# Host-laid feature-major memories, vectors and spatial weights, and a first layer that opens with the projections of raw memory

## Chip, core and metric

The kernel runs on one core of one Trainium2 chip. The metric is the device time in microseconds (us) of one execution. The engines are PE (TensorE), DVE (VectorE), ACT (ScalarE), POOL (GpSimd) and SP (SyncE, which here only issues DMA). The host prepares arrays before the launch; its time is not part of the metric.

## What is computed

Two blocks follow each other on 256 tokens of width 1024, two layers each. The part that matters here is the first block, and in it the branch that attends to a memory of 256 rows:

```python
def hybrid_layer(x, mem, ...):
    h = rms_norm(x, norm_pre)
    proj = h @ w_in                      # queries, keys, values, gates of five branches
    ...
    mkv = rms_norm(mem, mem_norm) @ w_mem_kv
    mem_k, mem_v = jnp.split(mkv, 2, axis=-1)
    y_xa = flat(memory_attention(heads(xa_q), heads(mem_k), heads(mem_v)))
    ...
def spatial_gating(u, v, ln_g, ln_b, w_s, b_s):
    mixed = jnp.einsum('gpq,bnqgc->bnpgc', jnp.where(mask, w_s, 0.0), vb)
```

`rms_norm(mem, g)` is, row by row, `mem * rsqrt(mean(mem^2) + eps) * g`. The factor of a row can be applied before or after the product with `w_mem_kv`. The second block has cross-attention to `mem_2` of the same form.

## The kernel before

**Products.** Every float32 weight is split in two fp32r parts, high and low, and a product is three passes: high x high, low x high, high x low. The host order `UNITS` cuts all weights into units of 512 KB. SP loads unit n into slot n mod 8 of `weights_raw` as soon as PE has finished unit n-8. ACT copies it to `weights_hi` (helper `emit`, L583); DVE subtracts and writes `weights_lo` into the same slot (L1056). PE takes the units in order. `proj_T` gives tokens on partitions (L1696), `proj_F` (L1728) and `proj_H` (L1761) features on partitions; in `proj_H` the sums of the two halves of a bank are taken by DVE (`both`, L1110).

**Order.** All four engines run straight lists written by hand; nothing reorders them. Where ACT or DVE wait for a bank (`filled`, `for_tile`) or for each other (`after_act`, `after_vec`), they first emit the splits of the units that their tables say are due:

```python
            def for_tile(name, i, stage=None):
                n, u = PC.split_at((name, i), stage), PC.unit_at((name, i), stage)
                while 0 < n < len(SPLITS) and SPLITS[n] < u + RAW - 2 and (n < SPLIT or SPLITS[n - SPLIT] < u - 1):
                    n += 1
                up_to(n)
```

So a wait inside ACT's list holds back all splits behind it, and SP's loads follow PE.

**Opening of layer 0.** SP loads `x` (two tiles of 512 KB), the identity, units 0 to 7, then 1184 KB of constants. PE runs 9 idle products on zeros (L1843), turns the 8 rows of `norm_pre` into columns (L1853), transposes the normalised tokens (L1815, `norm_T`) and starts on the queries `sbq` (L1728), the keys `sbk` (L1761), the gate columns `mlif` (L1870, L1871) and the values `sbv` (L1696). POOL loads some 40 small rows of vectors, which PE later turns into `vector_columns` (L1865) and `vector_columns_2` (L1929).

**Memory.** POOL loads `mem` as rows; ACT sums the squares (`square`, L621), DVE scales and adds eps (`base`, L1079), ACT takes Ln and Exp (`root`, L625, L627), DVE multiplies the rows (L1089). PE transposes 16 tiles (`turn`, L1801) to `memT`; ACT copies them and forms the high part of memory times `mem_norm`, DVE the low part (L1222). The key projection `mk` of layer 0 runs in the middle of the layer, the value projection `mv` behind `mlz`. Layer 1 does the same with `mem_2`, and the multiplied parts for the second layer and the second block come from `memT` (`mem_gains` L659, `mem_low` L1119). The spatial weights are a unit of 256 KB per layer that PE transposes (L1964).

## Time and profile before

| | |
|---|---|
| time, median of 3 runs | 1752.22 us (1751.6 to 1752.3) |
| span of the profiled execution | 1750.3 us |
| PE busy | 1740.1 us, 99% |
| DVE, ACT, POOL busy | 1283.1, 1024.5, 114.3 us |
| DMA | 306.64 MB, mean 175 GB/s |
| chain that ended last | PE 91%, DVE 6%, ACT 1% |

The only time given for the profiled execution is its span, from its first to its last instruction; the median lies 1.9 us above it, for what stands around the span. Busy shares are averages: the chain of waits tells which engine set the end in a stretch.

### The profile page before, as it was taken

The numbers are of one execution on the slowest core, as the hardware profiler recorded it, in microseconds if no ns is written. First come the engines' busy times: TensorE is split into PE (matmuls) and PEld (weight loads), VectorE is DVE, ScalarE is ACT, GpSimd is POOL, SyncE is SP. The second block draws the span as 40 slices with busy tenths as digits, with TensorE's granted clock in tenths as the row PEclk, the third lists the DMA queues.
The fourth block names the chain that finished last, engine by engine and source line by source line (L and its number), as shares of the span: only waits on it lengthen the run. The fifth ranks groups of instructions, "written<-read, shape, count | busy, mean of one in ns | idle before, by whom it ended". The sixth has DMA issues, their size and how long they took to land.

```text
span 1750.3 us, 24767 instructions
## 1 busy us (share of the span) xinstructions
PE 1740.1 (99%) x9406; PEld 1512.0 (86%) x9406; DVE 1283.1 (73%) x1714; ACT 1024.5 (59%) x1417; POOL 114.3 (7%) x186
## 2 busy tenths in 40 slices
PE   9999999999999999999999999999999999999998
PEld 8988898888889888888889988888888988888887
DVE  6966676665877586757669787688778987678775
ACT  7865566454666655644555765755556656555544
POOL 5000000000000000000000000500003360000000
PEclk9999999999999999999999999999999999999999
DMA  9656654566765566565666664456665515356663
GB/s 303 193 157 178 177 169 151 175 190 186 213 181 160 166 181 175 156 181 169 191 195 197 182 192 157 144 182 193 192 186 186 171 36 181 121 169 188 188 189 109
DMA packets 204070, 306.64 MB, mean 175 GB/s; under 512 B 12362, under 2 KB 100340, under 8 KB 203824
## 3 DMA queue, kind: packets, MB, share of 16 engines
q1 hardware_dynamic: 201056, 298.91, 56.1%
q0 software_dynamic: 2896, 6.15, 1.1%
q8 instruction: 75, 1.23, 0.3%
q14 instruction: 43, 0.35, 0.1%
HBM read 303.97 MB, written 1.05 MB: 174 GB/s over the span
## 4 chain that ended last, share of the span: by engine, by line
PE 91%; DVE 6%; ACT 1%; issue 1%; DMA 0%; DVEq 0%; ACTq 0%
PE bank L1696 52%; PE bank L1761 22%; PE bank L1728 8%; DVE bank L1573 2%; DVE weights_lo L1056 2%; PE bank L1801 1%; PE bank L1815 1%; PE bank L2093 1%; PE bank L2111 1%; PE bank L1823 1%; PE bank L1784 1%; ACT weights_hi L583 1%; PE bank L2017 0%; PE bank L1982 0%; PE bank L2065 0%
## 5 line engine op out<-in xcount | busy, mean ns | idle before, releaser
L1056 DVE TENSOR_TENSOR weights_lo<-weights_raw,weights_hi 128x1024 fp32r<-128x1024 f32 x560 | 668.9, 1233 | 248.6 <-ACT weights_hi L583 243.7
L583 ACT ACTIVATE weights_hi<-weights_raw 128x1024 fp32r<-128x1024 f32 x560 | 574.8, 1056 | 386.0 <-DMA weights_raw<-in_w_in_dram 181.3
L1696 PE MATMUL bank<-weights_hi,h_parts 128*128 128x512 f32 x1856 | 567.6, 391 | 0.4 <-DVE h_parts L1478 0.2
L1696 PEld LDWEIGHTS bank<-weights_hi,h_parts 128*128 128x128 f32 x1856 | 348.1, 188 | 73.3 <-DVE h_parts L1478 0.6
L1696 PE MATMUL bank<-weights_lo,h_parts 128*128 128x512 f32 x928 | 348.0, 390 | 0.0
L1696 PE MATMUL bank<-weights_hi,arena_parts 128*128 128x512 f32 x928 | 270.1, 391 | 0.0
L1761 PE MATMUL bank<-h_parts,weights_hi 128*128 128x512 f32 (+1 forms) x992 | 241.0, 385 | 0.5 <-DVE arena L1110 0.4
L1696 PEld LDWEIGHTS bank<-weights_lo,h_parts 128*128 128x128 f32 x928 | 174.4, 188 | 35.3
L1696 PEld LDWEIGHTS bank<-weights_hi,arena_parts 128*128 128x128 f32 x928 | 173.6, 188 | 35.4
L1761 PEld LDWEIGHTS bank<-h_parts,weights_hi 128*128 128x128 f32 x992 | 175.3, 189 | 31.8 <-DVE arena L1110 0.9
L1696 PE MATMUL bank<-weights_lo,arena_parts 128*128 128x512 f32 x464 | 158.4, 390 | 0.0
L1110 DVE TENSOR_REDUCE arena<-bank 128x256 f32<-128x512 f32 x148 | 102.1, 690 | 66.3 <-PE bank L1761 63.4
L1761 PEld LDWEIGHTS bank<-h_parts,weights_lo 128*128 128x128 f32 x992 | 134.8, 191 | 8.8
L1761 PE MATMUL bank<-h_parts,weights_lo 128*128 128x256 f32 x992 | 138.4, 283 | 0.0
L1728 PE MATMUL bank<-h_parts,weights_hi 128*128 128x256 f32 x768 | 133.7, 284 | 0.0
L1728 PEld LDWEIGHTS bank<-h_parts,weights_hi 128*128 128x128 f32 x768 | 116.3, 192 | 0.2 <-issue 0.2
L1696 PEld LDWEIGHTS bank<-weights_lo,arena_parts 128*128 128x128 f32 x464 | 87.2, 188 | 17.9
L1728 PE MATMUL bank<-h_parts,weights_lo 128*128 128x256 f32 x384 | 99.8, 284 | 0.0
L603 ACT ACTIVATE arena<-bank 128x512 f32<-128x512 f32 x140 | 83.0, 593 | 15.4 <-PE bank L1696 9.0
L1728 PEld LDWEIGHTS bank<-h_parts,weights_lo 128*128 128x128 f32 x384 | 69.7, 192 | 0.2 <-DVE weights_lo L1056 0.2
L960 ACT ACTIVATE arena<-arena,vector_columns 128x256 f32<-128x256 f32 x48 | 28.9, 602 | 64.7 <-DVE arena L1110 64.7
L541 POOL TENSOR_SCALAR arena<-constants_sb,vector_columns 128x128 f32<-128x128 f32 x76 | 35.4, 486 | 390.0 <-PE bank L1696 207.5
(326 smaller groups left out, 1667.6 us busy)
## 6 DMA issues: line engine op xcount, KB each, us to landing
weights_raw<-in_w_in_dram SPq DMA_DIRECT2D x224, 512.0 KB, 3.7
weights_raw<-in_f_w_up_dram SPq DMA_DIRECT2D x96, 512.0 KB, 3.5
weights_raw<-in_f_w_down_dram SPq DMA_DIRECT2D x48, 512.0 KB, 3.6
weights_raw<-in_w_up_dram SPq DMA_DIRECT2D x40, 512.0 KB, 3.5
weights_raw<-in_c_w_pw_dram SPq DMA_DIRECT2D x24, 512.0 KB, 3.6
weights_raw<-in_ab_w_in_dram SPq DMA_DIRECT2D x20, 512.0 KB, 3.8
weights_raw<-in_w_mem_kv_dram SPq DMA_DIRECT2D x16, 512.0 KB, 3.6
weights_raw<-in_w_out_dram SPq DMA_DIRECT2D x16, 512.0 KB, 3.6
```

Source lines behind the costliest of these rows:

```text
L541: ins = nc.gpsimd.tensor_scalar(diag(ft, d), ident, cols2[:, c:c + 1], 1.0, ALU.mult, ALU.mult)
L583: nc.scalar.activation(w_hi[:, q % SPLIT, 0:w], raw[:, n % RAW, 0:w], ACT.Copy).then_inc(hi_done, 1)
L603: link(nc.scalar.activation(dst, (view(b) if view else b[:, :]), func, **kw), ("free", name, i), *marks)
L960: link(nc.scalar.activation(c[:, f, :], feat(2)[:, f, :], ACT.Identity, scale=cols2[:, w0 + 48 + ft:w0 + 49 + ft], bias=cols2[:, b0 + ft:b ...
L1056: tt(w_lo[:, n % RAW, 0:w], raw[:, n % RAW, 0:w], w_hi[:, q % SPLIT, 0:w].bitcast(F32), ALU.subtract)\
L1110: link(nc.vector.tensor_reduce(dst, b, AX.X, ALU.add), ("free", name, f), f"{name}sum{f}")
L1573: stt(dst, feat(2, 2)[:, ft, 0:S - d], cols2[:, c:c + 1], acc[:, j, d:S], ALU.mult, ALU.add)\
L1696: return mm(bs[t][:, :], sp_[:, 2 * u + kk, t * P:(t + 1) * P], wp[:, kk, :], start=first and u == us[0] and kk == 0 and n == 0, stop=last ...
L1728: return mm(bs[i][:, j, :], wp[:, kk, f * P:(f + 1) * P], sp_[:, 2 * u + kk, :], start=first and u == us[0] and kk == 0 and n == 0 and j == 0,
L1761: return mm(out, w[n][:, kk, j * P:(j + 1) * P], sp_, start=u == 0 and kk == 0 and n == 0, stop=u == 1 and kk == 3, skip_group_check=True)
L1784: ins = mm(bs[j][:, 1, :], w[0][:, kk, j * P:(j + 1) * P], src[1][:, k, :], start=False, stop=u == 1 and kk == 3, skip_group_check=True)
L1801: ins = nc.tensor.transpose(b[:, j, t * P:(t + 1) * P], src[:, t, (2 * i + j) * P:(2 * i + j + 1) * P], ident)
```

## The change

The host now lays out seven arrays. `memT` and `mem_2T` are the memories with features first; `columns` and `columns_2` hold all vectors as columns, one load each; `gm_wsT` holds the spatial weights transposed. PE's transposes of these are gone, and so is the unit of spatial weights.

Layer 0 opens with `mk` and `mv` on raw memory times `mem_norm`. DVE forms both parts from three pieces of `memT`. The rows of `mem` are still loaded, for the mean squares alone. Their factors `mem_rstd` multiply the results: `mv` when ACT copies it out of its bank, `mk` on DVE after PE has spread the factors over all partitions (the new tile `mrs`, two small products a layer). DVE also multiplies `memT` itself with them (`memn`), for the later layers.

```diff
...
+        mem_rstd = [st[:, 11, t:t + 1] for t in range(NT)]
...
+            ORDER[f"L{l}"] = (four("mk") + (two("mv") if l == 0 else []) + four("hT") + two("sbq") + four("sbk") + pick("mlif", 0)
+                              + two("sbv") + pick("mrs", 0) + two("sbz") + (two("mv") if l else []) + four("sbs") + two("mlq", "mlk") + four("sbw") + two("mlv")
...
+                else:
+                    ap = kmaj("w_mem_kv", (l,))
+                    got.extend((True, ap[:, 4 * u:4 * u + 4, i * S:(i + 1) * S]) for u in range(2) for i in range(2))
+                    mem_v()
...
+            mT = A["memT"].rearrange("(k p) s -> p k s", p=P)
+            for i, (k0, k1) in enumerate(MEM_PIECES[:2]):
+                sp.dma_start(memT[:, k0:k1, :], mT[:, k0:k1, :]).then_inc(memT_in[i], 16)
             for n, (split, src) in enumerate(UNITS):
                 r = n % RAW
+                if n == 0:
+                    dst = raw[:, 0, 0:W].rearrange("p (k m) -> p k m", k=2)
+                    sp.dma_start(dst, src[:, 0:2, :]).then_inc(first_in, 16)
+                    dst = raw[:, 0, W:2 * W].rearrange("p (k m) -> p k m", k=2)
+                    sp.dma_start(dst, src[:, 2:4, :]).then_inc(raw_full[0], 16)
+                    continue
+                if n == 2:
+                    k0, k1 = MEM_PIECES[2]
+                    sp.dma_start(memT[:, k0:k1, :], mT[:, k0:k1, :]).then_inc(memT_in[2], 16)
+                if n == 4:
+                    for t, s in enumerate((x0_in, x1_in)):
+                        sp.dma_start(xs[:, t, :], A["x"][0][t * P:(t + 1) * P, :]).then_inc(s, 16)
+                    sp.dma_start(cst[:, 0:P], A["constants"][:, 0:P]).then_inc(ident_in, 16)
...
+            pool.dma_start(arena[:, 6:8, :], A["mem"][0].rearrange("(t p) d -> p t d", p=P)).then_inc(mem_in, 16)
...
+                    pool.dma_start(memT[:, :, :], A["mem_2T"].rearrange("(k p) s -> p k s", p=P)).then_inc(mem2T_in, 16)
...
+                    pool.dma_start(cols2[:, :], A["columns_2"]).then_inc(cols2_in, 16)
...
+                pool.dma_start(wsT[:, :, :], A["gm_wsT"][l]).then_inc(ws_in, 16)
...
+            def mem_norm(src):
+
+                for t in range(NT):
+                    for n in range(2):
+                        square(src[:, t, n * 512:(n + 1) * 512], "mem", t, n)
+                for t in range(NT):
+                    act.wait_ge(vec_done, after_vec(f"mem.base{t}"))
+                    link(nc.scalar.activation(mem_rstd[t], st[:, 8, 2 * t + 1:2 * t + 2], ACT.Ln, scale=1.0 / D, bias=st[:, 9, t:t + 1]))
+                    link(nc.scalar.activation(mem_rstd[t], mem_rstd[t], ACT.Exp, scale=-0.5), f"mem.rstd{t}")
...
+                    act.dma_start(cols[:, :], A["columns"]).then_inc(cols_in, 16)
+                    log_exp_table()
+                    up_to(4)
                     act.wait_ge(pool_done, GC.at("eps"))
-                    log_exp_table()
                     for t, s in enumerate((x0_in, x1_in)):
+                        up_to(4 + 2 * t)
                         act.wait_ge(s, 16)
                         link(nc.scalar.activation(sec(21), xs[:, t, :], ACT.Square, accum_out=st[:, 8, t:t + 1]))
                         link(nc.scalar.activation(st[:, 1, t:t + 1], st[:, 8, t:t + 1], ACT.Ln, scale=1.0 / D, bias=epsc))
                         link(nc.scalar.activation(st[:, 1, t:t + 1], st[:, 1, t:t + 1], ACT.Exp, scale=-0.5), f"h.rstd{t}")
-                    copy(cols[:, 0:8], "cols", 0, ACT.Copy, "gain", view=lambda b: b[:, 0:8])
-                    up_to(1)
...
+                    act.wait_ge(mem_in, 16)
+                    mem_norm(rows_of(6))
+                    for t in range(NT):
+                        copy(tok(5)[:, t, :], "mv", t, ACT.Copy, f"mv{t}", scale=mem_rstd[t])
...
+                    hi, lo = M_HL["L0"][:2]
+                    dve.wait_ge(cols_in, 16)
+                    for i, (k0, k1) in enumerate(MEM_PIECES):
+                        dve.wait_ge(memT_in[i], 16)
+                        for k in range(k0, k1):
+                            link(ts(hi[:, k, :], memT[:, k, :], cols[:, 8 + k:9 + k], None, ALU.mult))
+                        for k in range(k0, k1):
+                            link(stt(lo[:, k, :], memT[:, k, :], cols[:, 8 + k:9 + k], hi[:, k, :].bitcast(F32),
+                                     ALU.mult, ALU.subtract), f"m_lo{k}")
+                        if i == 1:
+                            up_to(2)
+                    up_to(4)
+                    all_of(feat(4), "mk", range(4), 2)
                 whole_norm(xs, xn, "h", "xn", based=True)
-                if l:
+                if l == 0:
+                    for t in range(NT):
+                        base("mem", t)
...
+                b = filled("mrs")[:, 0:S].unsqueeze(1)
                 if l == 0:
-                    hi, lo = M_HL["L0"][:2]
-                    for i in range(4):
-                        b = halves(filled("memT", i))
-                        for j in range(2):
-                            k = 2 * i + j
-                            dve.wait_ge(act_done, after_act(f"m_hi{k | 1}"))
-                            link(stt(lo[:, k, :], b[:, j, :], cols[:, 8 + k:9 + k], hi[:, k, :].bitcast(F32),
-                                     ALU.mult, ALU.subtract), *([("free", "memT", i), f"m_lo{i}"] if j else []))
+                    link(tt(feat(4), feat(4), b.to_broadcast([P, 4, S]), ALU.mult), "mk")
...
+                link(tt(memT[:, :, :], memT[:, :, :], b.to_broadcast([P, KD, S]), ALU.mult), "memn", ("free", "mrs", 0))
...
+                    elif opening:
+                        for kk in range(4):
+                            if at[0] == 1 and kk == 0:
+                                pe.wait_ge(first_hi, 1)
+                            if at[0] == 1 and kk == 2:
+                                pe.wait_ge(hi_done, 1)
+                            pe.wait_ge(vec_done, VC.at(f"m_lo{4 * u + kk}"))
+                            for j in range(2):
+                                part(j, kk, 0, bs[j].rearrange("p n s -> p (n s)"), src[2][:, 4 * u + kk].rearrange("p n s -> p (n s)"))
+                        low_half()
...
-                    idle(9)
+                    idle(6)
+                    for u in range(2):
+                        for i in range(2):
+                            proj_H("mk", i, M_HL["L0"], (u,), opening=True)
+                    proj_T("mv", src=M_HL["L0"])
...
-                m = rows_of(17 if l else 6)
-                pe.wait_ge(vec_done, VC.at("mem.n1"))
-                for i in range(4):
-                    turn("memT", i, m)
+                pe.wait_ge(act_done, SC.at("mem.rstd1"))
+                b = begin("mrs")
+                for t in range(NT):
+                    ins = mm(b[:, t * P:(t + 1) * P], mem_rstd[t].to_broadcast([P, P]), ident, start=True, stop=True)
+                end(ins, "mrs")
...
-                w = unit(4, P)
-                b = quarters(begin("wsT"))
-                for g in range(4):
-                    ins = nc.tensor.transpose(b[:, g, :], w[:, g, :], ident)
-                used(ins, ("wsT", 0))```

In the rows of order below, `weights_hi<-weights_raw` is ACT's split of a unit and `weights_lo<-weights_raw,weights_hi` DVE's. The first place is the opening on ACT. Before:

```order
L618 ACT_TABLE_LOAD
L675 ACTIVATE arena,statistics<-x_tokens 128x1024
L676 ACTIVATE statistics<-statistics 128x1
L677 ACTIVATE statistics<-statistics 128x1
L675 ACTIVATE arena,statistics<-x_tokens 128x1024
L676 ACTIVATE statistics<-statistics 128x1
L677 ACTIVATE statistics<-statistics 128x1
L603 ACTIVATE vector_columns<-bank 128x8
L583 ACTIVATE weights_hi<-weights_raw 128x1024
L654 ACTIVATE h_parts<-bank,vector_columns 128x256 x4
L583 ACTIVATE weights_hi<-weights_raw 128x1024
```

Now (L668 to L670 are the sums and factors of `x`, L600 the squares of `mem`, L624 and L625 its factors, L582 the copies of `mv`, L643 the high part of the tokens):

```order
L562 ACTIVATE weights_hi<-weights_raw 128x1024 x2
L668 ACTIVATE arena,statistics<-x_tokens 128x1024
L669 ACTIVATE statistics<-statistics 128x1
L670 ACTIVATE statistics<-statistics 128x1
L600 ACTIVATE spatial_weights,statistics<-arena 128x512 x4
L624 ACTIVATE statistics<-statistics 128x1
L625 ACTIVATE statistics<-statistics 128x1
L624 ACTIVATE statistics<-statistics 128x1
L625 ACTIVATE statistics<-statistics 128x1
L562 ACTIVATE weights_hi<-weights_raw 128x1024 x8
L582 ACTIVATE arena<-bank,statistics 128x512 x2
L643 ACTIVATE h_parts<-bank,vector_columns 128x256 x8
```

The first of these rows are units 4 and 5, the eight splits units 6 to 13: the squares and factors of memory now stand between unit 5 and unit 6, and units 6 to 13 ahead of the parts of the tokens.

The second place is the opening on DVE. Before:

```order
L1172 MEMSET arena 128x256
L1089 TENSOR_SCALAR arena<-x_tokens,statistics 128x1024
L1087 TENSOR_SCALAR arena<-x_tokens,statistics 128x512 x2
L1056 TENSOR_TENSOR weights_lo<-weights_raw,weights_hi 128x1024
L1104 SCALAR_TENSOR_TENSOR h_parts<-bank,vector_columns,h_parts 128x256 x4
```

Now, from the split of units 2 to 4 on (L1084 are the sums of `mk`, L1063 and L1061 the scaled tokens, L1053 the bases of memory's factors):

```order
L1030 TENSOR_TENSOR weights_lo<-weights_raw,weights_hi 128x1024 x3
L1084 TENSOR_REDUCE arena<-bank 128x256 x2
L1030 TENSOR_TENSOR weights_lo<-weights_raw,weights_hi 128x1024
L1084 TENSOR_REDUCE arena<-bank 128x256 x2
L1063 TENSOR_SCALAR arena<-x_tokens,statistics 128x1024
L1061 TENSOR_SCALAR arena<-x_tokens,statistics 128x512 x2
L1053 TENSOR_SCALAR statistics<-statistics 128x1 x2
L1030 TENSOR_TENSOR weights_lo<-weights_raw,weights_hi 128x1024 x8
```

The bases, for which ACT waits before its split of unit 6, stand behind all sums of `mk` and behind the scaled tokens.

## Rows read from the trace of the kernel before

**Rows 1.** The page: busy time of the engines, and the chain by engine.

```profile
PE 1740.1 (99%) x9406; PEld 1512.0 (86%) x9406; DVE 1283.1 (73%) x1714; ACT 1024.5 (59%) x1417; POOL 114.3 (7%) x186
...
PE 91%; DVE 6%; ACT 1%; issue 1%; DMA 0%; DVEq 0%; ACTq 0%
```

**Rows 2.** The chain from 0 to 60 us: start us, us, what.

```profile
1.19 6.42 PE bank L1843 x18
...
7.77 1.97 PE bank L1815 x16
...
21.84 11.20 PE bank L1761 x64
...
34.92 10.90 PE bank L1696 x48
45.82 1.75 PE bank L1801 x16
...
58.47 0.43 PE bank L1823 x2
58.91 0.22 PE bank L1824 x2
```

**Rows 3.** The chain from 146 to 148.5 us, and from 232.8 to 235.5 us.

```profile
146.99 0.83 PE bank L1929 x6
...
233.73 0.44 PE bank L1964 x4
```

**Rows 4.** In order of time from 466 to 513 us (layer 1); idle before in brackets.

```profile
509.44 1.54 DVE L1089 TENSOR_SCALAR arena<-arena,statistics 128x1024 f32<-128x1024 f32 x2 [0.54 <-ACT statistics L627]
...
511.04 1.97 PE L1801 MATMUL bank<-constants_sb,arena 128*128 128x128 f32 x16 [0.79 <-DVE arena L1089]
512.76 0.48 PE L1696 MATMUL bank<-weights_hi,h_parts 128*128 128x512 f32 x1
```

**Rows 5.** DMA from 0 to 40 us: GB/s of each us; issues: KB, us to landing.

```profile
GB/s 0 45 205 377 396 315 378 381 383 393 379 366 348 384 397 399 332 314 309 392 425 435 361 202 203 300 389 368 379 381 385 301 342 195 96 354 135 291 209 184
...
arena<-in_mem_dram POOLq DMA_DIRECT2D x1, 1024.0 KB, 8.3
```

**Rows 6.** DMA from 13 to 16 us, by queue: packets, MB, share of 16 engines.

```profile
q0 software_dynamic: 224, 0.88, 76.5%
q1 hardware_dynamic: 296, 0.30, 29.8%
```

**Rows 7.** ACT from 0 to 27 us in order of time.

```profile
4.46 1.06 ACT L675 ACTIVATE arena<-x_tokens 128x1024 f32<-128x1024 f32 x1 [2.32 <-DMA x_tokens<-in_x_dram]
...
18.58 1.06 ACT L583 ACTIVATE weights_hi<-weights_raw 128x1024 fp32r<-128x1024 f32 x1 [1.53 <-DMA weights_raw<-in_w_in_dram]
...
23.11 0.62 ACT L621 ACTIVATE spatial_weights<-arena 128x512 f32<-128x512 f32 x1
...
26.11 0.29 ACT L625 ACTIVATE statistics<-statistics 128x1 f32<-128x1 f32 x1
26.44 0.20 ACT L627 ACTIVATE statistics<-statistics 128x1 f32<-128x1 f32 x1
```

**Rows 8.** DVE from 0 to 62 us in order of time.

```profile
6.29 0.80 DVE L1089 TENSOR_SCALAR arena<-x_tokens,statistics 128x1024 f32<-128x1024 f32 x1 [5.15 <-ACT statistics L677]
8.02 1.01 DVE L1087 TENSOR_SCALAR arena<-x_tokens,statistics 128x512 f32<-128x512 f32 x2 [0.93 <-ACT statistics L677]
9.32 1.23 DVE L1056 TENSOR_TENSOR weights_lo<-weights_raw,weights_hi 128x1024 fp32r<-128x1024 f32 x1 [0.29 <-ACT weights_hi L583]
...
24.38 0.15 DVE L1079 TENSOR_SCALAR statistics<-statistics 128x1 f32<-128x1 f32 x1
...
30.71 1.41 DVE L1110 TENSOR_REDUCE arena<-bank 128x256 f32<-128x512 f32 x2
...
55.12 4.12 DVE L1222 SCALAR_TENSOR_TENSOR arena_parts<-bank,vector_columns,arena_parts 128x256 fp32r<-128x256 f32 x8
```

**Rows 9.** Groups of instructions by line: busy us, mean ns of one, idle before.

```profile
L1843 PE MATMUL bank<-arena 128*128 128x256 f32 x18 | 6.4, 536 | 1.2 <-DVE arena L1172 1.2
```

More of the change, by code:

```diff
@@ L136, in build @@
         wsT = sb("spatial_weights", [P, 4, P])
[L137 to L140 removed]
+        ident_r = sb("ident_parts", [P, P], F32R)
         cols = sb("vector_columns", [P, 104])
@@ L478, in _ @@
                         pool.dma_start(bif[32 * n:32 * n + H, l:l + 1], A[name][l].rearrange("(h a) -> h a", a=1)).then_inc(bif_in, 16)
-            pool.dma_start(arena[:, 6:8, :], A["mem"][0].rearrange("(t p) d -> p t d", p=P)).then_inc(mem_in, 16)
-            with nc.allow_non_contiguous_dma(reason="one position per partition"):
-                pool.dma_start(pos_i[:, :], A["positions"][0].rearrange("(t p) -> p t", p=P)).then_inc(pos_in, 16)
             def layer_rows(l):
@@ L1861, in layer @@
                 proj_F("sbq", **NORMED)
-                if l == 0:
-                    pe.wait_ge(rows_in, 10 * 16)
-                    b = begin("cols", 1)
-                    end(nc.tensor.transpose(b[:, 0:104], rows[0:104, :], ident[0:104, 0:104]), "cols", 1)
                 proj_W("sbk")
@@ L2243, with columns, laid_out @@
 COL_AB, COL_C, COL_F = 0, 80, (376, 496)
-ROWS2 = 25 * 16
-_INS = ["x", "mem", "positions", "norm_pre", "norm_post", "w_in", "b_igate", "b_fgate", "conv_q", "conv_k", "gm_ln_g",
-        "gm_ln_b", "gm_ws", "gm_bs", "mem_norm", "w_mem_kv", "w_up", "w_out", "mem_2", "ab_norm_2", "ab_w_in_2",
[4 rows of a table removed]
+_INS = ["x", "mem", "positions", "norm_post", "w_in", "b_igate", "b_fgate", "gm_ln_g",
+        "gm_ln_b", "w_mem_kv", "w_up", "w_out", "mem_2", "ab_w_in_2",
+        "a_gate_x_w_2", "a_gate_a_w_2", "b_group_w_2", "ab_w_out_2", "c_w_pw1_2",
+        "c_w_pw2_2", "c_b_pw2_2", "xa_wq_2", "xa_wk_2", "xa_wv_2", "xa_wo_2", "f_w_up_2", "f_w_down_2", "final_norm_2"]
+_LAID = ["memT", "mem_2T", "columns", "columns_2", "gm_wsT", "constants", "windows"]
+def columns(np, rows):
+    return np.concatenate([np.reshape(r, (-1, P)) for r in rows]).T
+def laid_out(np, inputs):
+    I = inputs
+    first, second = [], [I["ab_norm_2"][0], I["a_conv_w_2"][0], I["a_conv_b_2"][0], I["a_gate_x_b_2"][0], I["a_gate_a_b_2"][0],
+                         I["a_lambda_2"][0], I["b_group_b_2"][0], I["b_scale_2"][0],
+                         I["c_norm_2"][0], I["c_b_pw1_2"][0], I["c_dw_b_2"][0], I["c_ln_g_2"][0], I["c_ln_b_2"][0],
+                         I["c_dw_w_2"][0]]
+    for l in range(DEPTH):
+        first += [I["norm_pre"][l], I["mem_norm"][l], I["conv_q"][l], I["conv_k"][l], I["gm_bs"][l]]
+        second += [I["xa_norm_2"][l], I["xa_mem_norm_2"][l], I["f_norm_2"][l], I["f_dw_w_2"][l], I["f_dw_b_2"][l]]
+    got = {"memT": I["mem"][0].T, "mem_2T": I["mem_2"][0].T, "columns": columns(np, first),
+           "columns_2": columns(np, second), "gm_wsT": np.transpose(I["gm_ws"], (0, 3, 1, 2)),
+           "constants": constants(), "windows": windows()}
+    return {n: np.ascontiguousarray(got[n]) for n in _LAID}
 def kernel(**inputs):
```

171 lines of the change are left out of this document (45 added, 126 removed), and 4 rows, old and new, of the table _INS.

## The prediction

> **What bounds the kernel now.** I read the page first: PE is busy for 1740.1 of 1750.3 us, and the chain that ended last runs 91% on PE [rows 1]. A busy PE need not be a limiting PE, so I read the chain in order of time. From 7.77 us on it goes from one group of matmuls to the next without a gap as far as 60 us [rows 2]. Two things count here, then: what PE no longer executes, one for one, and any us in which PE stands still. The third view is the chain in layer 1. There it passes through DVE: the two steps of memory's scaling end at 509.44 + 1.54 = 510.98 us, and PE, idle for 0.79 us, then transposes [rows 4]. This is a wait in the middle of the kernel that the change can take away. Last come the DMA view and ACT's list for the first 35 us, since the new opening asks more of the loads than of PE.
>
> **Removed from PE behind the opening.** The 16 transposes of memory cost 1.75 us on the chain in layer 0 [rows 2]. In layer 1 the first transpose starts at 511.04 and the next product at 512.76, so 1.72 us, and the idle 0.79 goes with them [rows 4]: 2.51. It goes because PE now waits for ACT's factors, behind which DVE's 1.54 us of scaling began. The transposes of the spatial weights cost 0.44 us in each layer (one row shown, the other reads the same), and those of the second block's vectors 0.83 [rows 3]. Removed: 1.75 + 2.51 + 0.88 + 0.83 = 5.97 us; two single transposes of the first block's vectors are left out.
>
> **Added to PE.** `mrs` is two float32 products of 128 columns per layer. The trace has no product with a repeated stationary column. The nearest is L1824, the same size in float32, 0.22 us on the chain [rows 2]: 0.44 a layer, 0.88 in all. Below, it could be as short as a transpose, 1.75/16 = 0.11; above, 0.43 like 256 columns (L1823). I take 0.88; bounds 0.44 and 1.72. Net behind the opening: 5.1 us gained (4.2 to 5.5).
>
> **Moved.** `mk` and `mv` keep their matmuls. The four units of `sbk`, of the same form, took 11.20 us (L1761), 48 of `proj_T` 10.90 (L1696) [rows 2], together 22.1 us; they leave the middle and stand in front. The same shape is kept, so this is neutral unless PE stands still in them. The measure of the opening is therefore when `norm_T` starts, less 22.1, against 7.77 us before [rows 2].
>
> **The loads.** A load's landing is read from bytes. Up to the end of unit 4 the queues must bring memT 1.05 MB, units 0 to 4 2.62, `x` 1.05, the identity 0.07, `mem` 1.05 and the columns 0.05: 5.89 MB. Before, the rates of [rows 5] sum to 5.79 MB at 18.0 us and 6.10 at 19.0. Landings came later than their bytes: ACT got `x` tile 0 at 4.46 us, with 0.81 MB moved for its 0.52, and unit 5 at 18.58, with 5.97 moved for about 5.4 [rows 5, 7]. So between 0.3 and 0.6 MB overhang, and I allow up to 0.8. With 0.45, unit 4 lands when 6.34 MB are moved, at 19.6 us (18.9 to 20.6 by the overhang alone; 18.3 with none). The order of the queues matters little for this sum, but for unit 1 it does: while the rows of `mem` came in 4 KB pieces on POOL's queue beside SP's 1 KB pieces, POOL's had 0.88 MB of 1.18 [rows 6]. `mem` is now the first load of POOL, and 1.05 MB at 0.29 MB/us hold SP's queue down for some 3.6 us. Before, it landed 8.3 us after its issue [rows 5]; issued at 1.3 us it should do so by 9.6. Unit 1, not far behind unit 0, is then late and PE waits in `mk`; yet `mk`, 11.2 us long and begun at about 6, ends at 20.3 us even with 3 us of such waits, about when unit 4 comes. These waits are covered by unit 4.
>
> The Trainium skill, "DMA: Bandwidth & Descriptors", section "Queues, rings and completion order", says that each engine goes round between the queues that have work, a packet at a time; the 0.88 of 1.18 MB agrees with turns of unequal size. The same page's "Specifications" gives 435 GB/s as the fabric's ceiling; an estimate by that figure, with its fixed 2 us, would land unit 4 near 16.3 us, and the sum would be about that of rival D below.
>
> **The stall ahead of unit 6.** Counted from the landing L of unit 4: ACT splits it in 1.06 [rows 7], DVE in 1.23 [rows 8]; with issue gaps PE may start `mv` at L + 2.35. DVE then runs two sums (1.41), the split of unit 5 (1.2), two sums (1.41), the scaled tokens (0.80 + 1.01) and two bases (0.15 each) [rows 8]; with gaps it is at L + 8.6. ACT has by then done `x` tile 1 and the four squares of memory (from 23.11 to the Ln at 26.11, 3.0 us [rows 7]) and waits. Ln, Exp, Ln, Exp take 1.1, at 0.33 from Ln to Exp [rows 7], the split of unit 6 1.06, DVE's 1.23: unit 6 is ready at L + 12.05. PE has used up units 4 and 5 at L + 2.35 + 5.45 = L + 7.8. It stands still for 4.2 us. Units 6 and 7 take 5.45: `mv` ends at L + 17.5 = 37.1 us. The next thing due is already close: ACT's list has units 6 to 13 ahead of the copies of `mv` and of the tokens' high parts. Through unit 13 some 11.8 MB must come (units 7.34, constants 1.28, `x` 1.05, both forms of memory 2.10, columns 0.05); at 0.375 MB/us, the mean of the full stretches in [rows 5], beyond 7.35 MB at 22 us, that is 33.9, with overhang 35.1 us. Split and two copies later it is 37.4, so `sbq` can't start before about 37.9; through the stall it starts at 37.1 + 1.97 = 39.1. Without the stall only 1.2 us would come back.
>
> The opening then costs 37.1 - 22.1 - 7.77 = 7.2 us (bounds 5.9 with L = 18.3, and 8.2 with L = 20.6).
>
> **Edits costed at nothing.** DVE's new work in the body (`memn` over 2048 columns, `mk` over 1024, some 3 x 1.23 us) replaces 4.12 + 1.54 us [rows 4, 8] at the same place. The parts of raw memory on DVE (a low part like one of the eight of L1222, 0.5 us, a high part less [rows 8]) lie under the loads. The load of `mem_2T`, 1 MB, has some 100 us; if it held the weights back, unit after unit has seven slots of cover. The copies that ACT loses were hidden.
>
> **Sum.** 1750.3 + 7.2 - 5.1 = 1752.4 us of span, and with the 1.9 us between this span and the median **1754.3 us**. A measurement of this kernel can tell about 0.2%, 3.5 us, from no change. Likeliest: same, at +2.1 us; its own range is +0.4 to +4.0.
>
> **Rivals.**
> A, the clock. The granted clock reads 1.00 in every stretch, but the idle products at the start took 0.536 us each [rows 9], 6.42 us for 18 instructions, where L1823's pair, of the same size, takes 0.43 [rows 2]: 18 x 0.217 = 3.9. PE began at about half speed and paid 2.5 us for it. If the halt of 4.2 us throws it back to 1.2 GHz once, the sum is +4.6: 1756.8 us, slower. It decides from 1.4 us on. For it: the longest wait of PE in the rows is 1.2 us [rows 9], so nothing shows that it survives one. Against: four fifths of the opening are busy. The Trainium skill, "TensorE: Matmul & The Clock Gate", section "Why this matters for your kernels", asks for no longer idle gaps between bursts; by it this halt is a risk. Chance 0.15.
> B, loads slower than read: 1 KB rows, with `mem` against them, at nine tenths of the rate put unit 4 at 21.5 us and unit 13 at 38.8: +9.8 for the opening, +4.7 in all, 1756.9 us. Chance 0.13.
> C, a new wait in the body, such as `mrs` ahead of ACT's factors in layer 1 (they ended half a us ahead of the scaling, and PE needed them at 510.2) or weights behind `mem_2T`: +2 us more, 1756.3, at the edge of slower. Chance 0.08.
> D, loads that run near the row's peaks, 0.43 MB/us: unit 4 at 17 us, `mv` ends at 34.5, +4.6 for the opening, -0.5 in all: 1751.7, same. Chance 0.14.
> E, the other side: the opening hides as drawn. PE starts `mk` at about 5.9 and runs through, ACT's factors are in time; `norm_T` at 28.0, -1.9 and -5.1: 1745.2 us, faster. It decides where `sbq` starts before 33.4 us. Against it stand both the list of DVE and 11.8 MB by 31 us, 15% faster than the rows. Chance 0.10.
> Likeliest 0.40 (of it 0.03 beyond +3.5).
>
> **Numbers.** Faster 0.10; same 0.40 - 0.03 + 0.14 + 0.03 of C = 0.54; slower 0.15 + 0.13 + 0.05 of C + 0.03 = 0.36. The range for 8 in 10 leaves out E and the far ends of A and B: 1749 to 1759.
>
> **What would show it.** Right: PE idle for about 4 us before a unit of `mv` (L1681 there) with DVE's split as releaser; `norm_T` at 36 to 38 us; behind it the chain on PE, shorter by 5 us; no idle ahead of `mrs` at the place of 511 us. Wrong: `norm_T` before 33, or matmuls of `mv` at twice their length, or new idle of PE between 40 and 600 us.

## The result, and the profile after

The changed kernel takes 1769.19 us (median of 4 runs, 1767.9 to 1769.5) against 1752.01 before (4 runs): a ratio of 1.0097, with a 95% interval from 1.0082 to 1.0111. It is 17.2 us slower. Its profiled execution has a span of 1767.7 us, 17.4 more than before. The forecast was 1754.3, in 1749 to 1759.

The page first: instructions and busy time by engine.

```profile
span 1767.7 us, 24620 instructions
...
PE 1743.5 (99%) x9360; PEld 1512.8 (86%) x9360; DVE 1290.4 (73%) x1721; ACT 1016.2 (57%) x1398; POOL 99.8 (6%) x154
```

PE's share stays at 99%, as in [rows 1]. It even has 3.4 us more busy time, for less work: the first hint that some of its work ran slower. The list of waits of PE says where it stood still (what waited, for whom; total, times, longest, in us):

```profile
PE bank L1713 <- DVE h_parts L1078: 3.9, 1, 3.9
PE bank L1818 <- DVE mem_features L1210: 3.7, 1, 3.7
PE bank L1746 <- ACT weights_hi L551: 3.5, 1, 3.5
PE bank L1681 <- DVE weights_lo L1030: 3.0, 1, 3.0
PE bank L1838 <- DVE arena L1146: 1.2, 1, 1.2
PE bank L1746 <- ACT weights_hi L553: 0.9, 1, 0.9
```

Only the 1.2 us stood in the list of before. Of the others the 3.0 us ahead of unit 6 of the weights was forecast, and up to 3 us in `mk` were, as waits that cost nothing. Busy time by stretch shows what followed each wait (the last columns are the granted clock, the busy share of the DMA engines and GB/s):

```profile
10.00:16.00 6.00, 4.88 (x13) 3.59 (x14) 2.79 (x4) 1.83 (x3) 0.00 (x0) 0.53 1.09 367
34.00:38.00 4.00, 4.00 (x11) 3.16 (x12) 2.13 (x2) 4.00 (x5) 0.00 (x0) 0.57 0.15 52
49.00:55.00 6.00, 5.85 (x28) 5.86 (x29) 5.49 (x10) 0.26 (x1) 0.00 (x0) 0.52 0.10 7
553.00:557.00 4.00, 4.00 (x20) 3.86 (x20) 3.67 (x7) 3.78 (x8) 0.00 (x0) 0.57 0.00 0
```

Behind each of the four waits the granted clock is near 0.5, the lower of its two levels, 1.2 GHz. These four stretches are the whole difference in busy time and more.

Next, the same places of the chain in both kernels. Where `mk` and `mv` have moved to the front, their 22.1 us are added to the time of before. The first three times of before are in [rows 2]; the others are from the same view.

| place | before, + 22.1 us ahead of layer 0's old `mk` | after | later by |
|---|---|---|---|
| `norm_T` starts, layer 0 | 7.77 + 22.1 | 41.12 | 11.3 |
| `sbk` starts | 21.84 + 22.1 | 61.45 | 17.5 |
| scores of layer 0 | 58.47 + 22.1 | 96.76 | 16.2 |
| `sbz` starts, layer 1 | 513.00 | 525.30 | 12.3 |
| first products behind layer 1's scores | 537.42 | 554.20 | 16.8 |
| end of the span | 1750.3 | 1767.7 | 17.4 |

So the opening lost 17.5 us. The body gave back 5.2 as far as 525 us, and lost 4.5 at one place in layer 1 and 1.0 more in the products behind it (24.09 us for 192 that took 23.04).

ACT in the opening, in order of time (start, duration, idle before in brackets). L551 and L553 split the two halves of unit 0, L562 whole units:

```profile
9.52 0.63 ACT L551 ACTIVATE weights_hi<-weights_raw 128x512 fp32r<-128x512 f32 x1 [7.03 <-DMA weights_raw<-in_w_mem_kv_dram]
12.40 0.63 ACT L553 ACTIVATE weights_hi<-weights_raw 128x512 fp32r<-128x512 f32 x1 [2.25 <-DMA weights_raw<-in_w_mem_kv_dram]
13.31 1.06 ACT L562 ACTIVATE weights_hi<-weights_raw 128x1024 fp32r<-128x1024 f32 x1 [0.28 <-DMA weights_raw<-in_w_mem_kv_dram]
...
22.00 1.06 ACT L562 ACTIVATE weights_hi<-weights_raw 128x1024 fp32r<-128x1024 f32 x1 [1.14 <-DMA weights_raw<-in_w_mem_kv_dram]
...
31.48 7.69 ACT L562 ACTIVATE weights_hi<-weights_raw 128x1024 fp32r<-128x1024 f32 x8
```

Unit 0, the first thing that PE needs, is whole at 12.4 us; unit 4 is split at 22.00, where the forecast had 19.6. Who had the DMA engines meanwhile says the view by queue, from 3 to 9 us (q0 is POOL's queue, q1 SP's, q10 ACT's):

```profile
q0 software_dynamic: 345, 1.02, 54.1%
q1 hardware_dynamic: 946, 0.91, 46.4%
```

Memory's rows, wanted only for their squares, took half of the bytes. DVE from 26 to 60 us shows the two other waits of the opening:

```profile
30.10 0.34 DVE L1053 TENSOR_SCALAR statistics<-statistics 128x1 f32<-128x1 f32 x2
32.63 3.50 DVE L1030 TENSOR_TENSOR weights_lo<-weights_raw,weights_hi 128x1024 fp32r<-128x1024 f32 x3 [2.19 <-ACT weights_hi L562]
42.41 5.77 DVE L1030 TENSOR_TENSOR weights_lo<-weights_raw,weights_hi 128x1024 fp32r<-128x1024 f32 x5 [6.28 <-PE bank L1810]
48.10 4.12 DVE L1078 SCALAR_TENSOR_TENSOR h_parts<-bank,vector_columns,h_parts 128x256 fp32r<-128x256 f32 x8
```

The bases at 30.10 stand ahead of unit 6's low part at 32.63, as forecast. Then DVE is idle for 6.28 us behind its wait for `norm_T`, with five units unsplit whose high parts ACT had made by 39.2. It splits them first when `norm_T` is done, and `sbq`, which waits for the tokens' low parts behind them, goes on at 49.15.

Last, layer 1, DVE in order of time:

```profile
549.83 0.17 DVE L1202 TENSOR_TENSOR lambda_columns<-lambda_columns 128x8 f32<-128x8 f32 x1 [2.29 <-ACT lambda_columns L709]
...
550.45 2.29 DVE L1210 TENSOR_TENSOR mem_features<-mem_features,bank 128x2048 f32<-128x2048 f32 x1
```

and the chain there:

```profile
550.45 2.30 DVE mem_features L1210
552.74 0.04 issue
552.79 0.98 PE bank L1818 x2
553.77 0.43 PE bank L1819 x2
554.20 24.09 PE bank L1713 x192
```

`memn` reads the bank of `mrs`, and stands in DVE's list behind the wait for lambda's logarithm, which ACT gives late. The fourth group of scores wants that bank, so PE waits 3.7 us.

### The profile page after: what moved, and what is told of

Read it like the earlier page. It is cut to its first block, busy times and chain, and to the rows that moved or that the text cites. A ratio compares the mean times of both kernels' runs of the same rounds, so it can differ in the third digit from the quotient of the medians.

```text
span 1767.7 us, 24620 instructions
## 1 busy us (share of the span) xinstructions
PE 1743.5 (99%) x9360; PEld 1512.8 (86%) x9360; DVE 1290.4 (73%) x1721; ACT 1016.2 (57%) x1398; POOL 99.8 (6%) x154
## 3 DMA queue, kind: packets, MB, share of 16 engines
q8 instruction: 74, 1.21, 0.3%
## 4 chain that ended last, share of the span: by engine, by line
PE 93%; DVE 3%; ACT 1%; issue 1%; SPq 1%; DMA 1%; DVEq 0%; ACTq 0%
PE bank L1681 51%; PE bank L1746 21%; PE bank L1713 8%; PE bank L2148 3%; PE bank L2197 2%; DVE weights_lo L1030 1%; PE bank L1796 1%; PE bank L1810 1%; PE bank L2069 1%; PE bank L2087 1%; PE bank L1818 1%; PE bank L1779 1%; DMA weights_raw<-in_w_mem_kv_dram 1%; DVE arena L1084 0%; PE bank L1993 0%
## 5 line engine op out<-in xcount | busy, mean ns | idle before, releaser
L1030 DVE TENSOR_TENSOR weights_lo<-weights_raw,weights_hi 128x1024 fp32r<-128x1024 f32 x560 | 668.5, 1232 | 260.9 <-ACT weights_hi L562 244.8
L562 ACT ACTIVATE weights_hi<-weights_raw 128x1024 fp32r<-128x1024 f32 x559 | 574.5, 1056 | 397.9 <-DMA weights_raw<-in_w_in_dram 193.5
L1681 PE MATMUL bank<-weights_hi,h_parts 128*128 128x512 f32 x1856 | 567.0, 391 | 0.2
L1681 PEld LDWEIGHTS bank<-weights_hi,h_parts 128*128 128x128 f32 x1856 | 348.0, 188 | 73.0 <-DVE h_parts L1462 0.5
L1681 PE MATMUL bank<-weights_lo,h_parts 128*128 128x512 f32 x928 | 347.5, 389 | 0.0
L1681 PE MATMUL bank<-weights_hi,arena_parts 128*128 128x512 f32 x928 | 271.3, 392 | 3.0 <-DVE weights_lo L1030 3.0
L1746 PE MATMUL bank<-h_parts,weights_hi 128*128 128x512 f32 (+1 forms) x992 | 240.8, 384 | 0.5 <-DVE arena L1084 0.4
L1681 PEld LDWEIGHTS bank<-weights_hi,arena_parts 128*128 128x128 f32 x928 | 174.5, 189 | 39.2 <-DVE weights_lo L1030 3.4
L1681 PEld LDWEIGHTS bank<-weights_lo,h_parts 128*128 128x128 f32 x928 | 174.3, 188 | 35.4
L1746 PEld LDWEIGHTS bank<-h_parts,weights_hi 128*128 128x128 f32 x992 | 175.2, 189 | 31.9 <-DVE arena L1084 1.0
L1681 PE MATMUL bank<-weights_lo,arena_parts 128*128 128x512 f32 x464 | 158.9, 391 | 0.0
L1084 DVE TENSOR_REDUCE arena<-bank 128x256 f32<-128x512 f32 x148 | 102.0, 689 | 69.2 <-PE bank L1746 66.3
L1746 PEld LDWEIGHTS bank<-h_parts,weights_lo 128*128 128x128 f32 x992 | 134.7, 190 | 8.9
L1713 PE MATMUL bank<-h_parts,weights_hi 128*128 128x256 f32 x768 | 136.6, 288 | 4.0 <-DVE h_parts L1078 3.9
L1746 PE MATMUL bank<-h_parts,weights_lo 128*128 128x256 f32 x992 | 138.4, 282 | 0.0
L1713 PEld LDWEIGHTS bank<-h_parts,weights_hi 128*128 128x128 f32 x768 | 119.0, 197 | 4.4 <-DVE h_parts L1078 4.1
L1681 PEld LDWEIGHTS bank<-weights_lo,arena_parts 128*128 128x128 f32 x464 | 87.4, 188 | 18.1
L1713 PE MATMUL bank<-h_parts,weights_lo 128*128 128x256 f32 x384 | 100.8, 287 | 0.0
L582 ACT ACTIVATE arena<-bank 128x512 f32<-128x512 f32 x138 | 81.9, 593 | 16.7 <-PE bank L1681 8.2
L1713 PEld LDWEIGHTS bank<-h_parts,weights_lo 128*128 128x128 f32 x384 | 71.0, 196 | 0.0
```

Of the source, the lines that this page charges most:

```text
L562: nc.scalar.activation(w_hi[:, q % SPLIT, 0:w], raw[:, n % RAW, 0:w], ACT.Copy).then_inc(hi_done, 1)
L582: link(nc.scalar.activation(dst, (view(b) if view else b[:, :]), func, **kw), ("free", name, i), *marks)
L1030: tt(w_lo[:, n % RAW, 0:w], raw[:, n % RAW, 0:w], w_hi[:, q % SPLIT, 0:w].bitcast(F32), ALU.subtract)\
L1084: link(nc.vector.tensor_reduce(dst, b, AX.X, ALU.add), ("free", name, f), f"{name}sum{f}")
L1681: return mm(bs[t][:, :], sp_[:, 2 * u + kk, t * P:(t + 1) * P], wp[:, kk, :], start=first and u == us[0] and kk == 0 and n == 0, stop=last ...
L1713: return mm(bs[i][:, j, :], wp[:, kk, f * P:(f + 1) * P], sp_[:, 2 * u + kk, :], start=first and u == us[0] and kk == 0 and n == 0 and j == 0,
```

## The experiments

Each kernel was timed in five rounds beside the kernel before (1752.0 to 1752.3 in all of them). Edits are against the changed kernel or the kernel named; line numbers shift by a few between them. I give medians, and of a pair the difference.

**e1_memn_first**: `memn` in layer 1 ahead of lambda.

```diff
                 else:
+                    b = filled("mrs")[:, 0:S].unsqueeze(1)
+                    dve.wait_ge(mem2T_in, 16)
+                    link(tt(memT[:, :, :], memT[:, :, :], b.to_broadcast([P, KD, S]), ALU.mult), "memn", ("free", "mrs", 0))
                     dve.wait_ge(cols2_in, 16)
...
                     dve.wait_ge(act_done, after_act("lam.ln"))
...
-                else:
-                    dve.wait_ge(mem2T_in, 16)
```

> The changed kernel with one move on DVE in layer 1: the scaling of memory's features (memn, 2.30 us) stands ahead of the wait for the logarithm of lambda instead of behind it. Theory (the scaling is late only because it queues behind that wait, and holds the bank that the fourth group of scores wants): the wait of 3.72 us at 549 us goes and with it the half clock behind it (the next 192 products took 24.09 us, 1.05 more than in layer 0), so -4.8 us against the changed kernel, about 1764.4. Rival (DVE is simply full there; 2.3 us put earlier make a split of weights late): 0 to -1.5 us, with a new wait of PE for weights_lo between 525 and 549 us. Rival 2 (only the wait comes back, the clock falls anyway): -3.7.

Measured 1763.46 (1761.8 to 1764.2), -5.7. No wait is left there. The same edit on e4's successor gave -5.9 (e8 to e9 below) and on e6 -5.6 (to e7). In e8 the parts can be read: a wait of 3.7, then 0.70 for a product of the scores that takes 0.43 elsewhere [rows 2], and 24.53 for the 192 behind them, which take 23.04 in the kernel before. That is 3.7 + 0.3 + 1.5 = 5.5. The theory holds; the price of the half clock was set too low.

**e2_splits_early**: DVE makes the low parts of units 9 to 13 before it waits for `norm_T`.

```diff
             if C.stage == "L0":
+                if C is VC:
+                    return 6
                 return (1, 1, 2, 3)[i]
```

> The changed kernel, but in layer 0 DVE makes the low parts of units 9 to 13 before it waits for the transposes of the tokens, not behind them (it stood idle for 6.28 us ahead of 42.41 us and then did five splits, 5.8 us, before the first low part of the tokens). Theory: PE's wait of 3.9 us at 49.15 in sbq goes, and the half clock behind it (from 41.12, the start of the transposes, to 61.45, the start of sbk, it is 20.3 us against 14.1 in the kernel before): -6.3 us, about 1762.9. Rival (ACT's high parts, from 42.47 on, are the true bound of sbq): -1 to -2, PE then waits for ACT in sbq. Rival 2 (the clock does not come back with the wait): -3.9.

Measured 1762.86 (1761.9 to 1763.6), -6.3. On its chain `sbq` has no wait and runs at full clock:

```profile
41.51 1.75 PE bank L1812 x16
43.32 11.75 PE bank L1715 x96
55.07 10.93 PE bank L1748 x62
```

**e3_lists** and **e4_mem_late**: units 6 and 7 ahead of memory's factors, and then memory's rows behind unit 7 on SP's queue as well.

```diff
+                    up_to(8)
                     act.wait_ge(mem_in, 16)
                     mem_norm(rows_of(6))
...
+                if l == 0:
+                    up_to(8)
                 whole_norm(xs, xn, "h", "xn", based=True)
```

```diff
-            pool.dma_start(arena[:, 6:8, :], A["mem"][0].rearrange("(t p) d -> p t d", p=P)).then_inc(mem_in, 16)
...
                 if n == RAW:
+                    sp.dma_start(arena[:, 6:8, :], A["mem"][0].rearrange("(t p) d -> p t d", p=P)).then_inc(mem_in, 16)
```

> The changed kernel, with units 6 and 7 split on ACT before it turns to memory's squares, and on DVE before the scaled tokens and memory's bases; the loads are as they were. Theory (the wait ahead of unit 6 comes from the order of the lists, not from the landing of unit 6): the 3.0 us at 33.91 go, and the 1.9 us of half clock in units 6 and 7 (7.37 us for 24 products, 5.45 at full clock), -4.9 us, about 1764.3. Rival (what follows is gated by other things: the loads through unit 13, which ended at 35 us, and the five splits on DVE behind the transposes): 0 to -2, the time comes back as a longer wait in sbq.

> As e3_lists, and memory's rows (1 MB, for the squares alone) are loaded on SP's queue behind unit 7 instead of first of all on POOL's queue. Theory (they take the opening's bandwidth: unit 0 was split only at 9.52 us and unit 4 at 22.00): unit 0 lands near 7 us, unit 4 about 2.7 us earlier (1.05 MB at 0.385 MB/us), so -2.7 us against e3_lists, about 1761.6. Rival (SP's own issues hold the loads up, one took 4.19 us and two 3.09; the queue of POOL does not matter): 0 against e3_lists, the same slow issues at 4 to 12 us. Rival 2 (memory's factors now come late): a new wait of PE or ACT for memory's rows near 27 to 33 us, +1 to +3.

e3 measured 1762.28 (1760.8 to 1764.6), -6.9: the wait ahead of unit 6 is gone, so it came from the lists. That is two us more than expected. Its five runs spread over 3.8 us, and the profile, of a run of 1760.94, has unit 4 split at 20.25, with the loads as they were (e1's has 20.19, five other profiles with these loads 21.7 to 22.3). At `sbq` a wait of 3.1 us for ACT's high parts stands where the 3.9 for DVE's low parts stood. e4 measured 1761.21, 1.1 less than e3, where 2.7 was expected, and the ranges of the two overlap. Its trace says that the loads did what was expected and something else took it back:

```profile
5.79 0.63 ACT L551 ACTIVATE weights_hi<-weights_raw 128x512 fp32r<-128x512 f32 x1 [3.31 <-DMA weights_raw<-in_w_mem_kv_dram]
...
17.43 1.06 ACT L562 ACTIVATE weights_hi<-weights_raw 128x1024 fp32r<-128x1024 f32 x1 [1.14 <-DMA weights_raw<-in_w_mem_kv_dram]
...
36.15 1.06 ACT L562 ACTIVATE weights_hi<-weights_raw 128x1024 fp32r<-128x1024 f32 x1 [0.45 <-DMA weights_raw<-in_w_in_dram]
37.11 1.39 ACT L582 ACTIVATE arena<-bank,statistics 128x512 f32<-128x512 f32 x2
```

Against e3's profile, with unit 0 at 7.01 and unit 4 at 20.25, unit 0 comes 1.2 us earlier and unit 4 2.8, as expected; against the changed kernel's it is 3.7 and 4.6. But ACT's list holds the units through 13 ahead of the copies of `mv` (L582) and of the tokens' high parts, and unit 13 lands at 36.1. PE stood 6.4 us ahead of `sbq`, which starts at 39.15.

**e8_act_list** and **e9_act_list_memn**: e4 with ACT at most one unit ahead at the copies of `mv`; then with e1's edit.

```diff
                     for t in range(NT):
-                        copy(tok(5)[:, t, :], "mv", t, ACT.Copy, f"mv{t}", scale=mem_rstd[t])
+                        b = filled("mv", t, 1)
+                        link(nc.scalar.activation(tok(5)[:, t, :], b[:, :], ACT.Copy, scale=mem_rstd[t]), ("free", "mv", t), f"mv{t}")
```

> As e4_mem_late (mv ended near 31 us there, but PE then stood 6.4 us ahead of sbq, behind ACT, whose list has the splits of units 6 to 13 ahead of the copies of mv and of the tokens' high parts, and unit 13 landed at 36.12), with ACT going no further than unit 8 ahead of those copies. Theory (only the order of ACT's list holds sbq): sbq starts near 33.5 us instead of 39.15 and at full clock (14.46 us for its first 96 products there, 12.0 in the kernel before), so sbk at 46 to 47 instead of 53.6: -6.5 to -7.5 us against e4_mem_late, about 1754.2. Rival (the units 9 to 11 themselves come too late for sbq): waits for weights_hi in sbq, -3 at most, about 1758.

> As e8_act_list, with the scaling of memory's features ahead of the wait for lambda in layer 1 as in e1_memn_first. Theory (the terms add): 4.8 us less than e8_act_list, about 1749.5; against the kernel before the opening would then cost 2 to 3 us and the removed transposes give back 5.1, so a little faster than before. Rival (they do not add, since e1_memn_first took 5.7 and part of that was the opening): 1750 to 1752, the same as before.

e8 measured 1754.12 (11 runs), -7.1. e9 measured **1748.19** (11 runs, 1747.6 to 1749.3): 21.0 less than the changed kernel, and 0.9978 of the kernel before (0.9969 to 0.9986), faster than both. Its chain has no gap behind the opening:

```profile
19.62 11.12 PE bank L1686 x48
30.73 1.75 PE bank L1815 x16
32.48 0.06 issue
32.54 11.79 PE bank L1718 x96
44.33 11.17 PE bank L1751 x64
```

`sbk` starts at 44.33, where before with 22.1 us added is 43.94. The opening then costs 0.4 us, and the terms do add.

**e10_warm**: PE has work until `mk` can begin.

```diff
-                    idle(6)
+                    idle(18)
```

> The changed kernel with 18 idle products ahead of mk instead of 6, so that PE has work until about 8 to 9 us and the clock may stay up when mk begins. Theory (mk is covered by the landing of unit 4 and the order of the lists, so neither its late start nor its half clock costs anything): the same as the changed kernel, -1 to +0.5, and a longer wait ahead of unit 4 or unit 6. Rival (the half clock of mk, about 3 us of it between 10 and 18 us, is on the path): -3 us, about 1766.

Measured 1769.53, +0.3: no gain. The clock is 1.00 through `mk` there, and PE is done with units 4 and 5 earlier only to wait longer ahead of unit 6, until the same 33.6 us:

```profile
33.64 0.79 PE L1681 MATMUL bank<-weights_hi,arena_parts 128*128 128x512 f32 x1 [3.78 <-DVE weights_lo L1030]
```

So the half clock of `mk` costs nothing by itself in the changed kernel. Unit 0 is as late in e10 (9.74), so what its 3.5 us cost is not measured here; time won ahead of unit 6 went into the wait for it. What sets the end of that wait is unit 4 and the lists behind it.

**e12_mem_late_only**: the loads' edit of e4 without the lists'.

> The changed kernel with memory's rows on SP's queue behind unit 7 and the lists as they were, the part of e4_mem_late that concerns the loads alone. Theory (each part of e4 is hidden by the other and by what follows): mk starts near 6.5 us and unit 4 is split near 18, but the squares now wait for memory's rows until 25, and unit 6 is still behind them: ready near 32 instead of 33.9; sbq near 46 instead of 49.2: -2 to -3 us, about 1766.5. Rival (the loads alone are the cause): as e4_mem_late, 1761.

Measured 1766.51, -2.7, as expected. PE waited 5.1 us ahead of unit 6, until 31.25, and 3.9 us in `sbq` as before. The loads alone are worth little while the lists stand.

**e13_fill** and **e14_fill_half**: idle products of 256 columns in `sbq`, where PE waits for the tokens' low parts, 16 and then 8 of them. They add work that nothing uses.

```diff
+                        if u == 0 and PC.stage == "L0":
+                            pe.wait_ge(act_done, SC.at("mv1"))
+                            zeros = sec(16)[:, 0:S]
+                            for _ in range(16):
+                                mm(bank(PC, "mv", 0)[:, 0:S], zeros[:, 0:P], zeros, start=True, stop=True)
                         pe.wait_ge(vec_done, lo(u))
```

> The changed kernel with 16 idle products of 256 columns (3.5 us at full clock) on PE in sbq, at the place where it waits 3.9 us for the tokens' low parts; the wait stays, only PE is not idle in it. They add work that nothing uses. Theory (of the 6.3 us that the wait costs 3.9 are the wait and 2.4 the half clock behind it): the clock holds at 1.00 from 45 to 55 us, -2.4 us, about 1766.8. Rival (the clock falls for another reason than the idle stretch, or the products themselves push the end out): 0 or +1.

> As e13_fill with 8 idle products instead of 16. In e13_fill one product of 256 columns in float32 took 0.216 us a half and so 0.43 us in all, the 16 took 6.91 us where the wait was 3.9, and that pushed sbq's end out by as much as the held clock gave back (80 instructions of sbq behind it took 9.59 us, 12.30 in the changed kernel). 8 products are 3.45 us and lie inside the wait. Theory: the clock stays at 1.00 from 45 to 58 us, the 80 instructions take 9.6 to 9.8 us, -2.5 us against the changed kernel, about 1766.7. Rival (the fill only looked harmless: weights or banks behind it hold sbq anyway): 0.

e13 measured 1769.10, -0.1. It missed by my sizing: a float32 product is two instructions, so 16 of them took 6.91 us and overran the wait. e14 measured 1766.21 (1765.6 to 1767.4), -3.0. Its chain, with the splits and low parts of DVE as late as ever:

```profile
42.13 4.62 DVE weights_lo L1030 x4
46.75 0.41 DVE h_parts L1078
47.16 0.03 issue
47.18 0.49 DVE h_parts L1078
47.72 9.86 PE bank L1713 x80
```

The 80 instructions behind the wait take 9.86 us; in the changed kernel 12.30 (12.04 in e1, 12.13 in e12). The half clock behind that one wait costs 2.4 us by these rows. The 3.0 us of the whole time are no second measure of it, for the clock differed at two places that the edit does not touch. PE waited 3.5 us ahead of unit 6 here too, but the clock stayed at 1.00 behind it:

```profile
34.08 5.78 PE bank L1681 x24
```

```profile
34.00:36.00 2.00, 1.92 (x8) 1.60 (x9) 2.00 (x3) 2.00 (x3) 0.00 (x0) 1.00 0.35 114
```

These 24 took 7.37 us in the changed kernel. In layer 1, on the other hand, the 192 products behind the 3.7 us wait took 24.91 us instead of 24.09.

**e6_layout_only**, **e7_layout_memn**, **e11_layout_mem_late**: the host's layouts with the old opening. Memory's features are loaded behind `norm_T`, `memn` comes ahead of `angles`, and `mk` and `mv` are made of normed memory where they were. e7 adds e1's edit, e11 memory's rows behind unit 7.

```diff
-                    for u in range(2):
-                        for i in range(2):
-                            proj_H("mk", i, M_HL["L0"], (u,), opening=True)
-                    proj_T("mv", src=M_HL["L0"])
...
                 proj_T("mlv")
+                if l == 0:
+                    pe.wait_ge(vec_done, VC.at("m_lo7"))
+                    proj_W("mk", src=M_HL["L0"])
...
                 proj_T("mlz")
+                if l == 0:
+                    proj_T("mv", src=M_HL["L0"])
```

> The host's layouts without the new opening: layer 0 opens with the tokens as in the kernel before, mk and mv stand where they stood, memory's features come from the host and are scaled by mrs, the vectors and spatial weights come laid out. Theory (the removed transposes and the idle 0.79 give 5.1 us, and the scaling behind lambda's wait in layer 1 takes 4.8 of them): 1752.2 - 5.1 + 4.8 = 1751.9, the same as before. Rival (the transposes were worth nothing, since something else would hold PE): 1757 with the stall in layer 1. Rival 2 (the stall in layer 1 exists only by the shift of the opening): 1747.

> As e6_layout_only, with the scaling in layer 1 ahead of the wait for lambda. Theory: the whole 5.1 us, 1747.1, faster than both kernels by the interval. Rival (memory's features, 1 MB more, loaded in the first 100 us, make weights late in layer 0): a wait of PE for weights between 25 and 60 us and no gain.

> As e7_layout_memn, where unit 0 was split at 11.98 us (8.15 in the kernel before), PE stood 3.7 us ahead of sbq and ran at half clock behind it (14.36 us for 96 products, 12.0 before); here memory's rows leave the front of POOL's queue and go on SP's behind unit 7. Theory (memory's rows at the head of a second queue hold back what PE waits for first, in this opening too): unit 0 is split near 8.2, the wait goes and the clock holds, -6.1 us, about 1747.0, which is the kernel before less the 5.1 us of transposes and idle time. Rival (it is the columns on ACT's queue or memory's features that hold unit 0 back): no change, 1753.

e6 measured 1758.60, e7 1753.01, e11 1750.82 (11 runs, 1749.9 to 1752.5; 0.9995 of before, 0.9986 to 1.0003). They are 6.7, 5.9 and 3.8 us above what I expected, and the traces say why. In e7 unit 0 is split at

```profile
11.98 1.06 ACT L547 ACTIVATE weights_hi<-weights_raw 128x1024 fp32r<-128x1024 f32 x1 [3.96 <-DMA weights_raw<-in_w_in_dram]
```

for with the row loads of the vectors gone from POOL's queue, memory's rows moved up to its head there too. PE waited 3.7 us and ran at half clock behind it, and no row of my expectation for e6 had that. In e11 the same row reads 8.93, PE waits 0.6 us, and the clock holds. But it has a new wait of 1.9 us for `weights_lo` between 60 and 100 us, which I put down to my own placing of `memn` and the low parts of memory on a full DVE; no run tests that. Its span is 1748.4: 1750.3 - 5.1 + 0.6 + 1.9 = 1747.7, and 0.7 that I did not trace.

## Why the prediction was wrong

The direction of the likeliest case, slower opening and shorter body, was right. The size of the opening was not, and the place in layer 1 was costed at nothing. Against the forecast sum of +2.1 the span has +17.4, so 15.3 us to explain.

**The loads (+2.4).** The overhang was put at 0.45 MB, at most 0.8. Unit 4 was split at 22.00 with 6.98 MB moved for its 5.89, an overhang of 1.1. Part of that is the single profile: the seven with this opening (the changed kernel, e1, e2, e3, e10, e13, e14) have unit 4 between 20.19 and 22.25, at 21.5 on the mean. The step also said that "the order of the queues matters little for this sum". The four profiles with memory's rows behind unit 7 (e4, e8, e9, e12) have it between 17.18 and 18.17, at 17.7 on the mean: 3.8 us earlier, where the rows' 1.05 MB at 0.385 MB/us are only 2.7. (The step's own bounds are a little off too: overhangs of 0.3 and 0.8 MB give 19.2 and 20.5 us by its rates, not 18.9 and 20.6.)

**The stall ahead of unit 6 (right; -0.1).** The working gave unit 6 at L + 12.05, and with L = 22.00 it came at 33.91, L + 11.9. Its cause, the order of the lists, is shown by e3. The wait was 3.0 instead of 4.2, because PE was later too; the waits ahead of and in `mk`, 4.4 us in all, were covered, as said, for PE still had to wait behind them.

**The clock in units 6 and 7 (+1.8).** From 33.91 to `norm_T` at 41.12 are 7.2 us against 5.45. This is rival A, which had 0.15. It was right in its mechanism and "once" was its error: each of the waits of 3.0 to 3.9 us in the changed kernel was followed by a stretch near 0.5. Not every wait does it: ahead of unit 6 PE waited 2.0 us in e13's profile and 3.5 us in e14's, and behind both the clock read 1.00 from 34 to 38 us. What decides it these runs do not show. The Trainium skill, "TensorE: Matmul & The Clock Gate", section "Why this matters for your kernels", asks for no long idle gaps between bursts; the four stretches shown above agree, e14's wait of 3.5 us does not. The rival deserved more than 0.15, since the likeliest case itself contained a wait of 4.2 us.

**Between `norm_T` and `sbk` (+6.3).** The forecast had nothing here: "through the stall it starts at 37.1 + 1.97". It read that ACT's list holds units through 13 ahead of the tokens' high parts, and did not follow DVE's list behind it, which waits for ACT's marks with all the units that ACT has passed. Five splits, 5.77 us, stood between `norm_T` and the first low part. Of the 6.3 us 3.9 are the wait and 2.4 the clock (e14); e2 took all of it away, -6.3. This step failed worst: the prediction asked of ACT's list what was due next ("The next thing due is already close") and did not ask it of DVE's.

**`memn` in layer 1 (+5.5).** The edit costed at nothing, which "replaces 4.12 + 1.54 us at the same place", was wrong in the place. The old scaling stood ahead of lambda's wait in DVE's list, the new one stands behind it, and it holds a bank that PE wants. Rival C had a new wait in the body at +2 us and another spot, `mrs`; its waiting there was nil. e1 measures it at 5.7, e8 and e9 at 5.9.

**What was removed (-0.5, right).** The sum gave 5.1 in all, of which 0.4 lies behind layer 1's scores. The table shows 5.2 us won between `sbk` and 525 us. Half of the 0.5 is in layer 1, where the chain takes up the next product at 513.00 and not at the 512.76 of [rows 4]; the rest I did not trace. `mrs` takes 0.44 for its four instructions, as taken. e9 carries the proof: with the opening at +0.4, its span is 4.5 below the kernel before.

The terms: 2.4 - 0.1 + 1.8 + 6.3 + 5.5 - 0.5 = 15.4. They come from one profile; those of the loads and of the clock would differ by a us or two in another.

**Rival E** had 0.10 and was judged to need loads 15% faster. It said that it decides where `sbq` starts before 33.4 us. e9 starts it at 32.54 with nearly the same rates (10.43 MB moved by 30 us, 10.18 in the changed kernel): not the loads but three list orders and the place of one load stood against it.

## What to carry to other kernels

When work moves to the front of an engine's list, follow every list that waits for marks in it (here ACT's, then DVE's behind it) as far as the first thing that PE needs, and where a wait of PE as long as those here (3.0 to 3.9 us) comes out, reckon with the half clock behind it (1.5 to 2.9 us here, and nothing once, in e14). Ask of each load that is now first in any queue who needs it first: removing small loads from POOL's queue was enough to move 1 MB in front of what PE waited for. And a step that releases a bank is not free just because an equal step was: look at what stands ahead of it in its list, and at who wants the bank.
